# Where the first two conditioning chunks stand in TensorE's order of an attention

## The reference

```python
# first block, selected and windowed branch of every head
s = einsum(qq, keys) * scale ; p = softmax(where(valid, s, MASK)) ; o = p @ values
# second block, layer l, for both condition vectors (c and c_ctx)
mod_x = (silu(c) @ w_ada[l] + b_ada[l]).reshape(bn, 1, N_MOD, d)
mod_c = (silu(c_ctx) @ w_ada[l] + b_ada[l]).reshape(1, 1, N_MOD, d)
o_a = _neighbourhood_attn(q_a, k_a, v_a, k_a_c, v_a_c, na_rpb[l])
o_b = _pool_mix(p_x[..., OFF_B_U:OFF_C_Q], pool_w[l], pool_scale[l])
o_c = _gqa_blocks(q_c, concatenate([k_c, k_c_c]), concatenate([v_c, v_c_c]))
```

## Time and profile before

| | us |
|---|---|
| three runs | 2240.62, 2242.02, 2242.71; median 2242.02 |
| the profiled execution's own time | 2245.0 |
| its span, first to last instruction | 2243.7 |
| TensorE busy | 2135.7 (95%) |
| VectorE busy | 1073.4 (48%) |
| ScalarE busy | 770.6 (34%) |
| GpSimd busy | 58.5 (3%) |
| mean granted TensorE clock | 0.972 |

### The profile page before, as it was taken

The page is one execution under the profiler, slowest core; times in us unless marked ns, Lnnn a source line. Parts: engine busy times, 40 slices in busy tenths (PEclk is TensorE's granted clock), DMA queues, the critical chain, the costliest instruction groups (busy, mean ns, idle before and its releaser), DMA issues.

```text
span 2243.7 us, 40849 instructions
## 1 busy us (share of the span) xinstructions
PE 2135.7 (95%) x17742; PEld 1834.4 (82%) x17742; DVE 1073.4 (48%) x1568; ACT 770.6 (34%) x1094; POOL 58.5 (3%) x59
## 2 busy tenths in 40 slices
PE   7997889998999999989999999999999999999998
PEld 6886689997888887867778888878888888688997
DVE  5654665555333334566453333354333346755555
ACT  5421444343221233236342222233222224354433
POOL 0000020000000000120000000000000000200000
PEclk9999899998999999999999999999999999899999
DMA  7516644542433323328522232232232225364543
GB/s 280 198 60 242 216 155 168 190 162 105 158 145 107 103 74 117 91 94 275 198 76 88 91 112 93 78 120 78 87 108 94 90 88 131 111 229 144 178 170 110
DMA packets 56626, 303.56 MB, mean 135 GB/s; under 512 B 13728, under 2 KB 17184, under 8 KB 27552
## 3 DMA queue, kind: packets, MB, share of 16 engines
q1 hardware_dynamic: 56480, 301.40, 39.4%
HBM read 300.33 MB, written 1.05 MB: 134 GB/s over the span
## 4 chain that ended last, share of the span: by engine, by line
PE 85%; DVE 8%; ACT 4%; issue 1%; DMA 1%; ACTq 0%; SPq 0%; DVEq 0%
PE ps L458 22%; PE ps L460 21%; PE ps L459 21%; DVE w_lo L445 3%; PE ps L573 3%; PE ps L574 3%; PE ps L577 3%; PE ps L487 3%; ACT w_hi L439 3%; PE ps L1853 1%; PE ps L1842 1%; PE ps L1606 1%; PE ps L1834 1%; DVE mx L1945 1%; DMA raw<-in_w_ada 1%
## 5 line engine op out<-in xcount | busy, mean ns | idle before, releaser
L458 PE MATMUL ps<-a_hi,w_hi 128*128 128x512 f32 (+1 forms) x1992 | 685.7, 344 | 2.4 <-DVE w_lo L445 2.4
L459 PE MATMUL ps<-a_lo,w_hi 128*128 128x512 f32 (+1 forms) x1992 | 679.2, 341 | 0.0
L460 PE MATMUL ps<-a_hi,w_lo 128*128 128x512 f32 (+1 forms) x1992 | 678.9, 341 | 0.0
L445 DVE TENSOR_TENSOR w_lo<-raw,w_hi 128x2048 fp32r<-128x2048 f32 (+2 forms) x230 | 469.8, 2046 | 241.0 <-ACT w_hi L439 240.6
L439 ACT ACTIVATE w_hi<-raw 128x2048 fp32r<-128x2048 f32 (+2 forms) x229 | 391.2, 1715 | 257.9 <-PE ps L460 172.1
L458 PEld LDWEIGHTS ps<-a_hi,w_hi 128*128 128x128 f32 x1992 | 378.8, 190 | 49.5 <-issue 3.8
L460 PEld LDWEIGHTS ps<-a_hi,w_lo 128*128 128x128 f32 x1992 | 378.7, 190 | 42.4
L459 PEld LDWEIGHTS ps<-a_lo,w_hi 128*128 128x128 f32 x1992 | 378.8, 190 | 42.1
L458 PE MATMUL ps<-ff_hi,w_hi 128*128 128x512 f32 (+1 forms) x880 | 306.4, 348 | 6.7 <-DVE w_lo L445 6.7
L459 PE MATMUL ps<-ff_lo,w_hi 128*128 128x512 f32 (+1 forms) x880 | 304.9, 347 | 0.0
L460 PE MATMUL ps<-ff_hi,w_lo 128*128 128x512 f32 (+1 forms) x880 | 304.9, 346 | 0.0
(11 more groups left out here) (352 smaller groups left out, 1802.3 us busy)
## 6 DMA issues: line engine op xcount, KB each, us to landing
raw<-in_w_gu SPq DMA_DIRECT2D x110, 1024.0 KB, 4.8
raw<-in_w_ada SPq DMA_DIRECT2D x72, 1024.0 KB, 5.6
raw<-in_w_dn SPq DMA_DIRECT2D x80, 704.0 KB, 4.1
raw<-in_w_in SPq DMA_DIRECT2D x26, 1024.0 KB, 5.0
raw<-in_w_out SPq DMA_DIRECT2D x12, 1024.0 KB, 5.1
direct<-in_w_cmp SPq DMA_DIRECT2D x4, 1024.0 KB, 7.6
h<-in_x SPq DMA_DIRECT2D x2, 1024.0 KB, 7.0
nb<-in_rpb SPq DMA_DIRECT2D x32, 64.0 KB, 6.3
```

Of the source, the lines that this page charges most:

```text
L445: nc.vector.tensor_tensor(w_lo[slot][:, cols], raw[b][:, cols], w_hi[slot][:, cols].bitcast(F32), ALU.subtract).then_inc(lo_ready if done ...
L458: nc.tensor.matmul(banks[m], w1, a1, start=start and k == 0, stop=False)
L459: nc.tensor.matmul(banks[m], w1, a2, start=False, stop=False)
L460: last = nc.tensor.matmul(banks[m], w2, a1, start=False, stop=stop and k == pr.kt - 1)
```

## The change

TensorE's loop in `pe_attend` issues the first two conditioning chunks of each attention at step 2, both ahead of the scores of job 2, where chunk 0 was issued at step 3 and chunk 1 at step 4, each behind that step's scores. The wait for the pooling's two counts moves with them. Steps 3 and 4 issue no chunk; chunk 2 and the later ones stay where they were, at step a + 3. Nothing else differs: the same instructions, banks, loads and drains.

```diff
         for t in range(n + 3):
+            if t == 2:
+                if key != "first":
+                    pe.wait_ge(pr_dve, qd(key, "pool"))
+                    pe.wait_ge(pr_act, qa(key, "pool"))
+                inner_ada(pe, key, 0)
+                inner_ada(pe, key, 1)
             if t < n:
                 scores(j0 + t, jobs[t])
-            if 3 <= t < inners[key].inner[1] + 3:
-                if key != "first" and t == 3:
-                    pe.wait_ge(pr_dve, qd(key, "pool"))
-                    pe.wait_ge(pr_act, qa(key, "pool"))
+            if 5 <= t < inners[key].inner[1] + 3:
                 if t % 2:
                     wait(pe, at_olo, (j0 + t - 3) // 2 - 1)
                 inner_ada(pe, key, t - 3)
```

## The result

| | before | after |
|---|---|---|
| median of 20 runs of each, side by side | 2241.24 us | 2247.54 us |
| ratio of the two | | 1.0022, 95% interval 1.0012 to 1.0032 |
| the profiled execution, its span | 2245.0, 2243.7 us | 2245.85, 2244.6 us |

By the ratio the changed kernel is 0.22% slower, about 5 us (2.7 to 7.2); the two medians lie 6.3 us apart, which is within that interval. A second comparison, made later, gave 1.0020 (1.0007 to 1.0033). The forecast was +2.6 us, 2244.6. The mechanism behind layer 0's part was found as forecast at step 5; the first block's part was missing from the sum, and layer 1 lost its time in another way than forecast.

The account below looks back on a forecast made before the run. The prediction took TensorE, 85% of the chain, to bound the kernel. Layer 0's 1.1, layer 1's 1.2, the first block's 0 and 0.3 for its bounds gave +2.6 us, forecasting 2244.6 us; range 2240.0 to 2248.4.

Parts of the forecast that it names:

- the likeliest case: All three attentions: moving the pair costs +1.3 to +4.5 us, giving 2243.3 to 2246.5 us; chance 0.55.
- the third rival: Steps 3 and 4, without chunks: TensorE's clock falls, 1 to 2.5 us an attention, 2248.1 us in all; chance 0.18.
- Layer 0, job 2's delay: Layer 0's start: late scores delay VectorE by 2.34 us, then ScalarE's `pt` and TensorE's transposes; layer ends 1.1 us later.
- Lost at the start is carried whole to the end: Each attention: with TensorE never idle in layer 0's steady 4.14 us step, start losses or gains last to the end.
- The faster rival: Gaps at the layers' starts: filling them saves 2.0 us (2240.0), or gives 2236.5 with full clock earlier; chance 0.12.
- Layer 1: Layer 1's start: VectorE gets job 2's scores 1.1 to 2.35 us late; loss 0.4 to 1.7 us, taken as 1.2.
- the second rival: Layer 1's start: idle stretch of 2.9 instead of 3.7 us keeps the clock; +0.4 us, 2242.4; chance 0.15.
- First block: First block's start: late scores are swallowed by the 3 us `nm` stall; 0 us, or 0 to 1.5 at low clock.
- The rule on idle gaps: TensorE's gaps between bursts of matmuls: a filled gap keeps or brings back the clock, giving 2236.5 us.
- Loads: First block: three chunk loads go out together, chunk 2 landing by 250.3 at worst, before its need at 252.24; cost nothing.
- The sum: All three attentions: 1.1 + 1.2 + 0 us, plus 0.3 for the first block's bounds, makes +2.6 us.

Follow-up runs that it names:

- work in the gap: Kernel before with extra unread matmuls ahead of job 2's scores, one chunk's worth in the first block and three in each layer: 1.0010 (0.9996 to 1.0024).
- the pair in the gap: Kernel before with the pooling's result in banks 4 and 5 and, in the layers only, the two chunks ahead of job 2's scores: 1.0009 (0.9997 to 1.0022).
- the control with the banks alone: Kernel before with the pooling's product in banks 4 and 5 and nothing else moved: 1.0007 (0.9992 to 1.0022).

## Why the prediction was right or wrong

- **The number: within the range, in part by luck.** The measured median, 2247.54 us, lies in the stated range (2240.0 to 2248.4) but above the likeliest case's own (2243.3 to 2246.5), and the rise of about 5 us is twice the 2.6 forecast. It is nearest to the third rival, the clock falling in the thinned steps (2248.1, chance 0.18), and in the first block and in layer 1 the traces show this rival's mechanism. The range held the result because that rival set its upper end, not because the sum was right.
- **Layer 0, job 2's delay: right in mechanism and size.** Forecast: the pair can't use the gap, scores 3.7 us after the pooling step (3.6), VectorE idle about 2.2 us (2.12), step 5's scores 16.5 us after the pooling step (16.4), 1.1 us later in all. Step 5 was 1.0, 0.9 and 1.0 us later than before in the three profiles that have the edit there, and the loss was gone with the pair behind the scores (20.37) and with one chunk (20.82).
- **"Lost at the start is carried whole to the end": borne out in layer 1, hidden by something else in layer 0.** In layer 1, the stretch from step 5 to the end took 37.17 or 37.18 us in six of the seven executions without a break in it, the changed kernel's among them (the seventh, with work in the gap, took 37.77), so there a loss at step 5 is carried whole. In layer 0 more was lost than the 1.0. The ends are 100.23, 101.82 and 99.94 us where layer 0 was changed, and 97.62, 97.45, 98.16 and 98.65 where it was not, a difference of 2.7 us in the mean. The rest lies in breaks inside runs of small matmuls near the end, and in matmuls at half speed behind the longest of them, both described below. They occur with the change and without it, and layer 0 alone measured only +0.4 us (-1.6 to +2.2), so whether the change makes them longer stays open.
- **The faster rival: its mechanism came, its gain did not.** The full clock did come back sooner in layer 0, at 999.53 directly behind job 2's scores, where before even the next chunk was slow. The prediction's argument against it held: VectorE's delay follows from the scores alone. Its condition, job 2's scores ended by 1001.0 or 10.4 us after job 0's, was met in the run with added matmuls in steps 3 and 4 (9.9 us, and full speed from there on): step 5 came at 21.09, no better than before. Work in the gap and the pair in the gap had 21.02 and 21.08.
- **Layer 1: near in size in the profiles, wrong in cause.** Forecast 1.2 us, from VectorE getting job 2 late by 1.1 to 2.35 us (the quick case is 0.9 by the prediction's own terms, 1951.44 + 1.86 + 1.4 + 1.1 against 1954.94, and its loss 0.2, not 0.4). Measured: VectorE was not late at all, 8.43 us in the kernel before and in all three profiles with the edit. The scores started 1.15 us later but, at 1.13 instead of 2.08 us, ended only 0.2 us later, because the 2.94 us gap kept the clock, as the second rival had it, which would have made the layer lose nothing. But the steps without chunks lost it, which is the third rival: 21.4 us at step 5 in two profiles and 19.86 in one, with the same idle time in front, where unchanged ones had 19.55 to 20.34. By time layer 1 alone cost nothing that can be seen, -0.7 us (-2.7 to +1.3).
- **First block: the term that fell short.** The step of the prediction reads "a scores step late by under 2 us is swallowed there, and the chunks taken from steps 3 and 4 were hidden in the same waits. So 0 is my value". The first half held: VectorE did not wait. The second did not. The hidden chunk was the only work TensorE had in that wait, and with it gone the transposes, values, scores and chunk 2 ran at half speed for 15 us. Step 5 came at 21.03 to 21.61 us in three profiles with the edit and at 19.64 to 20.23 in six without, step 6 at 26.78 to 28.29 against 23.71 to 24.30; by time the first block alone costs 2.0 us (0 to 4.3). The bound of 1.5 us that the prediction named "if the clock is low" was nearly the value itself; the 0.3 us it put in the sum was not. That the lost clock is the cause rests on these timelines and on the pair behind the scores; the runs with added matmuls did not settle it.
- **The rule on idle gaps.** The granted clock of the first block's attention is 0.78, 0.81 and 0.75 in the three profiles with the emptied steps, and 0.81 to 0.92 in six without. The Trainium skill (TensorE: Matmul & The Clock Gate, "Why this matters for your kernels") advises against idle gaps between bursts of matmuls. The trace agrees for the first block, where the pair closes the gap of 1.86 us in front and opens one of 2.87 us behind, after which matmuls run at half speed. It does not agree for layer 1's gap of 2.94 us, which was followed by full speed. The prediction used it for the faster rival alone.
- **Loads: right.** The three loads in the first block went out together at 239.2 to 240.0 and landed by 248.90, before chunk 2 at 251.54.
- **The sum.** Means of the ends over the profiles with and without the edit give +1.4 us for the first block (47.1 and 45.7, three and six profiles), +2.7 for layer 0 and +1.4 for layer 1 (58.9 and 57.4, three and four), together 5.5 us, beside about 5 measured. The executions differ by up to 3 us in one attention, and the three kernels with one attention changed add up to less (1.0008), so the shares are rough and stay open. The forecast had 0.3, 1.1 and 1.2.

No version measured here is clearly faster than the kernel before.

## What to carry to other kernels

Before filling an idle stretch, ask two things of the timeline: when the filler itself may start, and what idle time it leaves at the place it came from. A piece of work that is "hidden" in a wait can still be paying for itself by holding TensorE's clock, so moving it away isn't free. And an engine that is never idle in a steady step may still be only level with a chain through other engines: take a piece of its work out and see whether the step gets shorter.

## What the runs showed of the hardware

- **Full speed after one kind of gap and not after another.** A break of 2.94 us was followed by full-speed matmuls in layer 1, one of 2.87 us in the first block by 15 us at half speed, and the same 2.32 us by slow scores (1.22 us) in one execution and quick ones (0.70) in another. The length of the break before them alone does not tell.
- **Breaks inside runs of small matmuls.** Near the end of layer 0's attention, TensorE stops in the middle of a chunk of 64 matmuls, with nothing to wait for that the profile shows ("issue"):

```profile
1081.58 0.85 PE L487 MATMUL ps<-raw,silu_c 128*32 128x64 f32 x19 [1.89 <-issue]
```

  The kernel before has 1.02 us at this place, three other executions with layer 0 unchanged 1.56, 1.61 and 1.83, the control with the banks alone 1.89; with the edit there, 1.89, 1.71 and 2.51. No run was made for the cause, but the traces point to one. They list some 116 transfers of 16 KB each in a DMA queue called "instruction". All 48 breaks over 0.3 us of this kind between 225 and 2010 us, over the 14 profiles, end 1.25 to 1.59 us after one of these transfers has landed. So TensorE appears to wait there for its next instructions, though most of the transfers come without a break. In 7 of the 14 profiles the longest break near layer 0's end was 1.71 to 2.51 us and the granted clock fell to half around its end; in the other 7 it was 1.02 to 1.61 us and the clock stayed full.
- **One VectorE instruction stands still beside GpSimd.** `nm`, four columns wide, takes 0.17 us alone (at 233.41 in the changed kernel) and 3.04 us when it starts during GpSimd's subtraction, and in other runs 3.04 to 3.08. The Trainium skill (Trainium Architecture — The Big Picture, "What this means for kernel authors") says that the two engines share a pair of ports under an exclusive lock; the trace agrees for `nm`, which ends when GpSimd's instruction does. Not every VectorE instruction is held: the scaling at 234.68 and the maximum behind it start during the same subtraction and take 0.69 us each, as without it (229.29 and 230.01).
